# Expert gates: one-hot matrices built for 16 tokens at a time, token innermost, by bf16 tensor-tensor operations

## What is computed

```python
v1, i1 = lax.top_k(s1, PEER_TOPK_HALF)
v2, i2 = lax.top_k(s2, PEER_TOPK_HALF)
cand = (v1[..., :, None] + v2[..., None, :]).reshape(PEER_CHUNK, PEER_HEADS, -1)
cand_idx = (i1[..., :, None] * N_KEYS + i2[..., None, :]).reshape(PEER_CHUNK, PEER_HEADS, -1)
top_s, pos = lax.top_k(cand, PEER_TOPK)
experts = jnp.take_along_axis(cand_idx, pos, axis=-1)
gate = jax.nn.softmax(top_s.astype(jnp.float32), axis=-1).astype(hc.dtype)
u = jnp.take(expert_u, experts, axis=0)
act = jax.nn.gelu(jnp.einsum('chkd,cd->chk', u, hc))
v = jnp.take(expert_v, experts, axis=0)
return jnp.einsum('chk,chkd->cd', gate * act, v)
```

## Time and profile before

| | |
|---|---|
| median of three runs | 3415.33 us |
| lowest and highest | 3412.12, 3416.04 us |
| profiled execution, span from its first to its last instruction | 3404.0 us |
| median of the runs less that span | 11.3 us |
| TensorE busy in the span | 3128.4 us (92%) |
| VectorE busy | 2179.6 us (64%) |
| ScalarE busy | 1150.9 us (34%) |
| GpSimd busy | 1267.2 us (37%) |
| mean granted TensorE clock, share of full | 0.977 |

### The profile page before, as it was taken

One profiled execution on the slowest core, in us unless ns is written; L12 is line 12 of the kernel. 1 busy time (PEld: TensorE's weight loads), 2 busy tenths in 40 slices (PEclk: granted clock), 3 DMA queues, 4 the chain that ended last, 5 costly groups with the idle time before them and its releaser, 6 DMA issues.

```text
span 3404.0 us, 46182 instructions
## 1 busy us (share of the span) xinstructions
PE 3128.4 (92%) x14602; PEld 2508.8 (74%) x14602; DVE 2179.6 (64%) x4512; ACT 1150.9 (34%) x1478; POOL 1267.2 (37%) x513
## 2 busy tenths in 40 slices
PE   5888999998999999979999977788789999999998
PEld 3777788775678887757788866666668788888886
DVE  7973555133356623964169999999991566666664
ACT  3344322245332223323332234344443222222222
POOL 3313444432144444424434432222224344444442
PEclk8989999999999999989999999999999999999999
DMA  8411454421145442212234433444435555555552
GB/s 322 170 38 62 160 197 169 140 68 62 38 143 188 179 158 88 81 62 90 90 103 147 139 123 141 155 142 148 152 133 204 167 181 191 197 197 188 191 188 75
DMA packets 170247, 482.32 MB, mean 142 GB/s; under 512 B 15360, under 2 KB 48896, under 8 KB 168080
## 3 DMA queue, kind: packets, MB, share of 16 engines
q1 hardware_dynamic: 147680, 410.83, 35.6%
q10 hardware_dynamic: 22448, 70.14, 5.3%
HBM read 411.70 MB, written 69.21 MB: 141 GB/s over the span
## 4 chain that ended last, share of the span: by engine, by line
PE 41%; issue 35%; DVE 12%; POOL 10%; DVEq 1%; ACT 1%; DMA 0%; POOLq 0%; SPq 0%; ACTq 0%
PE ps L1614 39%; POOL w_lo L545 10%; DVE oh_key L1547 2%; DVE oh_gate L1544 2%; DVE oh_gate L1545 2%; PE pa L1614 2%; DVE oh_gate L1546 2%; DVE s_acc L1410 1%; DVE e_t L1568 1%; DVEq L1544 0%; DMA e_g<-expert_act 0%; DVE s_tmp L1461 0%; DVEq L1407 0%; DVE s_pb L1422 0%; DVE mg_lo L1463 0%
## 5 line engine op out<-in xcount | busy, mean ns | idle before, releaser
L545 POOL TENSOR_TENSOR w_lo<-raw,w_hi 128x1024 fp32r<-128x1024 f32 x509 | 1267.0, 2491 | 2105.7 <-ACT w_hi L562 2105.5
L1614 PE MATMUL ps<-h_hi,w_hi 128*128 128x512 f32 x2392 | 954.4, 399 | 43.8 <-ACT h_hi L641 36.9
L1614 PE MATMUL ps<-h_hi,w_lo 128*128 128x512 f32 x2392 | 942.9, 394 | 0.0
L1614 PE MATMUL ps<-h_lo,w_hi 128*128 128x512 f32 x2392 | 918.1, 391 | 0.0
L562 ACT ACTIVATE w_hi<-raw 128x1024 fp32r<-128x1024 f32 x509 | 537.6, 1058 | 718.3 <-PE ps L1614 593.4
L1614 PEld LDWEIGHTS ps<-h_hi,w_hi 128*128 128x128 f32 x2392 | 457.1, 191 | 147.2 <-issue 42.0
L1614 PEld LDWEIGHTS ps<-h_hi,w_lo 128*128 128x128 f32 x2392 | 455.7, 191 | 96.8
L1614 PEld LDWEIGHTS ps<-h_lo,w_hi 128*128 128x128 f32 x2392 | 452.6, 189 | 93.7 <-issue 1.7
L1614 PE MATMUL ps<-wa_hi,w_hi 128*128 128x512 f32 x1024 | 404.9, 395 | 5.7 <-DVE wa_lo L1571 5.7
L1614 PE MATMUL ps<-wa_lo,w_hi 128*128 128x512 f32 x1024 | 409.7, 400 | 0.0
L1614 PE MATMUL ps<-wa_hi,w_lo 128*128 128x512 f32 x1024 | 402.4, 393 | 0.0
(11 more groups left out here) (314 smaller groups left out, 3586.5 us busy)
## 6 DMA issues: line engine op xcount, KB each, us to landing
ada<-in_ada SPq DMA_DIRECT2D x144, 512.0 KB, 5.0
raw<-in_expert_u SPq DMA_DIRECT2D x128, 512.0 KB, 3.8
raw<-in_expert_v SPq DMA_DIRECT2D x128, 512.0 KB, 4.5
raw<-in_ffn_in SPq DMA_DIRECT2D x88, 512.0 KB, 4.2
expert_act<-g_act ACTq DMA_DIRECT2D x128, 256.0 KB, 3.1
gate_matrix<-w_st ACTq DMA_DIRECT2D x16, 2048.0 KB, 6.6
e_w<-gate_matrix SPq DMA_DIRECT2D x16, 2048.0 KB, 11.3
e_g<-expert_act SPq DMA_DIRECT2D x128, 256.0 KB, 8.0
```

Of the source, the lines that this page charges most:

```text
L545: nc.gpsimd.tensor_tensor(w_lo[:, k, :], raw[:, k, :], w_hi[:, k, :].bitcast(F32), ALU.subtract)\
L1614: return nc.tensor.matmul(out, a, b, start=start, stop=stop_)
```

## The change

The one-hot matrices are made for 16 tokens at once. The buffers are laid out [key, token] instead of [token, key], two buffers of 16 tokens each (`OHB`, `OHT`). For each 16 tokens VectorE compares an expanded iota with the first keys (`oh_hit`) and with the second keys (`oh_key`), both broadcast over the 128 keys, then multiplies `oh_hit` by each of the three gate parts. All operands are bf16; keys and gate parts are kept as bf16 (`r_key`, `r_gate`). TensorE waits for `oh_ready` once in 16 tokens, and both its operands now step over 16 elements (`[:, b, :, t]`, `[:, b, a, :, t]`). `oh_hits` orders the multiplications behind the comparison. `OH_FREE` is 8 groups, that is two buffers of 16 tokens.

```diff
@@ -59,7 +59,8 @@
 NG = NK // GE
 ADA0 = 8
 WTOK = 32
-OHG = 4
+OHT = 16
+OHB = 2
 U_FIRST, U_GATES = 44, 64
 U_LAST = NK - U_FIRST - U_GATES
 
@@ -273,11 +274,12 @@
     r_q = ar("r_q", 0, [2 * PH, S])
     w_st = ar("w_st", 0, [2, NK, WTOK])
     r_s = ar("r_s", 32 * K, [TT, 2 * PH, NK])
-    oh_gate = ar("oh_gate", 32 * K, [4 * OHG, 3, NK], BF16)
-    oh_key = ar("oh_key", 44 * K, [4 * OHG, NK], BF16)
-    r_rest = ar("r_rest", 48 * K, [S])
-    r_part = ar("r_part", 50 * K, [S], BF16)
-    iota_b = ar("iota_b", 51 * K, [NK], BF16)
+    oh_gate = ar("oh_gate", 32 * K, [OHB, 3, NK, OHT], BF16)
+    oh_key = ar("oh_key", 56 * K, [OHB, NK, OHT], BF16)
+    oh_hit = ar("oh_hit", 64 * K, [OHB, NK, OHT], BF16)
+    iota_t = ar("iota_t", 72 * K, [NK, OHT], BF16)
+    r_key = ar("r_key", 76 * K, [2, S], BF16)
+    r_gate = ar("r_gate", 78 * K, [3, S], BF16)
     r_w = ar("r_w", 64 * K, [2 * PH, NK])
     r_oh = ar("r_oh", 64 * K, [PH, TK, TK])
     r_cand = ar("r_cand", 72 * K, [PH, TK * TK])
@@ -293,7 +295,7 @@
     r_z = ar("r_z", 92 * K, [2, TT, PH])
 
     g_act = at("g_act", ada_off, [2, S])
-    r_T = at("r_T", ada_off + 4 * K, [4, S])
+    r_T = at("r_T", ada_off + 4 * K, [2, S])
 
     wa_hi = ar("wa_hi", 0, [2, GE, S], F32R)
     wa_lo = ar("wa_lo", 32 * K, [2, GE, S], F32R)
@@ -356,7 +358,7 @@
         sem(n) for n in ("mix_done", "pw_mm", "pmh", "pml", "mgh", "mgt", "mg_done"))
     rs_mm, rs_out, top_done, gx_done, gate_done, rt_mm, rt_done = (
         sem(n) for n in ("rs_mm", "rs_out", "top_done", "gx_done", "gate_done", "rt_mm", "rt_done"))
-    oh_ready, wb_mm, wb_free = (sem(n) for n in ("oh_ready", "wb_mm", "wb_free"))
+    oh_hits, oh_ready, wb_mm, wb_free = (sem(n) for n in ("oh_hits", "oh_ready", "wb_mm", "wb_free"))
     act_st = [sem(f"act_st{i}") for i in range(2)]
     w_out_st = [sem(f"w_out_st{i}") for i in range(2)]
     e_w_in = sem("e_w_in")
@@ -926,6 +928,8 @@
     assert U_FIRST % RING == U_GATES % RING == U_LAST % RING == 0
     WPER = 2 * U_GATES // (S // WTOK)
 
+    OH_FREE = OHB * OHT // 4
+
     def act_peer(act, hi):
         m, T = M0["query"], T0["query"]
         act.wait_ge(h_ready, 6 * DT)
@@ -955,8 +959,9 @@
             hi.upto(m + k + 3)
             act_gelu(act, 0, RING, m, T, k, 0)
         act.wait_ge(rt_mm, 1)
-        for a in range(3):
-            nc.scalar.activation(r_T[:, a, :], pa[:, a, :], ACT.Copy).then_inc(rt_done, 1)
+        for a in range(2):
+            nc.scalar.activation(r_key[:, a, :], pa[:, a, :], ACT.Copy).then_inc(rt_done, 1)
+        nc.scalar.activation(r_T[:, 0, :], pa[:, 2, :], ACT.Copy).then_inc(rt_done, 1)
         act.wait_ge(rt_done, 3)
         nc.scalar.activation(r_z[:, 0, 0, 0:1], r_z[:, 1, 0, 0:1], ACT.Copy).then_inc(wb_free, 4)
         for k in range(U_FIRST - RING // 2, U_FIRST):
@@ -972,7 +977,7 @@
                 n = WTOK // 4 // (WPER // 2)
                 for q in range(n * (k % (WPER // 2)), n * (k % (WPER // 2)) + n):
                     g = WTOK // 4 * b + q
-                    act.wait_ge(wb_mm, i * (2 * WTOK // 4) + (OHG + g + 1))
+                    act.wait_ge(wb_mm, i * (2 * WTOK // 4) + (OH_FREE + g + 1))
                     if q == 0 and not isinstance(i, int):
                         act.wait_ge(w_out_st[b], i * 16)
                     nc.scalar.activation(w_st[:, b, :, 4 * q:4 * q + 4].rearrange("p n t -> p t n"),
@@ -1526,32 +1531,31 @@
         step(v.reciprocal(z1, z0))
         v.tensor_tensor(e, e, bc(z1, 2, TK), ALU.mult).then_inc(gate_done, 1)
 
-        step(v.tensor_copy(iota_b[:, :], iota))
+        v.tensor_copy(iota_t[:, :, :], bc(iota, 2, OHT))
         dve.wait_ge(rt_done, 3)
-        step(v.tensor_copy(r_part[:, :], r_T[:, 2, :]))
-        step(v.tensor_tensor(r_T[:, 3, :], r_T[:, 2, :], r_part[:, :], ALU.subtract))
-        step(v.tensor_copy(r_part[:, :], r_T[:, 3, :]))
-        step(v.tensor_tensor(r_rest[:, :], r_T[:, 3, :], r_part[:, :], ALU.subtract))
-
-        per = 2 * WTOK // 4
+        step(v.tensor_copy(r_gate[:, 0, :], r_T[:, 0, :]))
+        step(v.tensor_tensor(r_T[:, 1, :], r_T[:, 0, :], r_gate[:, 0, :], ALU.subtract))
+        step(v.tensor_copy(r_gate[:, 1, :], r_T[:, 1, :]))
+        step(v.tensor_tensor(r_T[:, 0, :], r_T[:, 1, :], r_gate[:, 1, :], ALU.subtract))
+        step(v.tensor_copy(r_gate[:, 2, :], r_T[:, 0, :]))
+
+        per = 2 * WTOK // OHT
         with dve.Fori(0, S // (2 * WTOK)) as i:
-            for g in range(per):
-                dve.wait_ge(wb_mm, i * per + (g + 1))
-                for j in range(4):
-                    s = g % OHG * 4 + j
-                    tok = i * (2 * WTOK) + (4 * g + j)
-                    key1, key2, gate, less1 = (r_T[:, a, bass.ds(tok, 1)] for a in range(4))
-                    v.tensor_scalar(oh_gate[:, s, 0, :], iota_b[:, :], key1, gate, ALU.is_equal, ALU.mult)
-                    v.tensor_scalar(oh_gate[:, s, 1, :], iota_b[:, :], key1, less1, ALU.is_equal, ALU.mult)
-                    v.tensor_scalar(oh_gate[:, s, 2, :], iota_b[:, :], key1, r_rest[:, bass.ds(tok, 1)], ALU.is_equal, ALU.mult)
-                    ins = v.tensor_scalar(oh_key[:, s, :], iota_b[:, :], key2, None, ALU.is_equal)
+            for n in range(per):
+                b, tok = n % OHB, bass.ds(i * (2 * WTOK) + OHT * n, OHT)
+                dve.wait_ge(wb_mm, (i * per + (n + 1)) * (OHT // 4))
+                v.tensor_tensor(oh_hit[:, b, :, :], iota_t[:, :, :], bc(r_key[:, 0, tok], 1, NK), ALU.is_equal).then_inc(oh_hits, 1)
+                v.tensor_tensor(oh_key[:, b, :, :], iota_t[:, :, :], bc(r_key[:, 1, tok], 1, NK), ALU.is_equal)
+                dve.wait_ge(oh_hits, i * per + (n + 1))
+                for a in range(3):
+                    ins = v.tensor_tensor(oh_gate[:, b, a, :, :], oh_hit[:, b, :, :], bc(r_gate[:, a, tok], 1, NK), ALU.mult)
                 ins.then_inc(oh_ready, 1)
 
     def dve_peer(dve):
         v = nc.vector
         dve_router(dve)
         m, T = M0["expert_v"], T0["expert_v"]
-        dve.wait_ge(wb_mm, OHG + S // 4)
+        dve.wait_ge(wb_mm, OH_FREE + S // 4)
 
         def gated(g, k, b, i=None):
 
@@ -1981,7 +1985,7 @@
             for t in range(TT):
                 last = nc.tensor.transpose(pa[:, a, t * P:(t + 1) * P], r_i[:, a, t, :], ident)
                 if a == t == 0:
-                    last.then_inc(wb_mm, OHG)
+                    last.then_inc(wb_mm, OH_FREE)
         last.then_inc(rt_mm, 1)
         for k in range(U_FIRST - RING // 2, U_FIRST):
             first(m, T, k, 0, RING)
@@ -1991,12 +1995,13 @@
                 first(m, T, k, i, WPER)
                 n = 2 * WTOK // 4 // WPER
                 for g in range(n * k, n * k + n):
-                    pe.wait_ge(oh_ready, i * (2 * WTOK // 4) + (g + 1))
+                    if 4 * g % OHT == 0:
+                        pe.wait_ge(oh_ready, i * (2 * WTOK // OHT) + (4 * g // OHT + 1))
                     pe.wait_ge(wb_free, i * (2 * WTOK // 4) + (g + 1))
                     for j in range(4):
-                        s, out = g % OHG * 4 + j, pa[:, g % 4, j * NK:(j + 1) * NK]
+                        b, t, out = 4 * g // OHT % OHB, (4 * g + j) % OHT, pa[:, g % 4, j * NK:(j + 1) * NK]
                         for a in range(3):
-                            last = mm(out, oh_key[:, s, :], oh_gate[:, s, a, :], a == 0, a == 2)
+                            last = mm(out, oh_key[:, b, :, t], oh_gate[:, b, a, :, t], a == 0, a == 2)
                     last.then_inc(wb_mm, 1)
         m, T = m + U_GATES, T + U_GATES
         with pe.Fori(0, U_LAST // RING) as i:
```

## The result

The changed kernel takes 3713.89 us (median of four runs, 3711.86 to 3716.56) against 3413.72 for the kernel before, run beside it four times: a ratio of 1.0881, 95% interval [1.0868, 1.0894]. It is slower by 300 us. The prediction had it slower too, but by 125 us.

A forecast was written before the change was run, and what follows sets the result against it. VectorE was taken to bound the 572.3 us gate stage. With strided gate matmuls TensorE would need 1536 x 0.227 + 1536 x 0.227 = 697 us, +125 on the median 3415.33, giving 3540 us; range 3345 to 3650.

The forecast's parts named there:

- What bounds the kernel before: Gate stage: VectorE sets the pace, busy 560.80 of 572.30 us; TensorE needs 433, so 139 us is the most to gain.
- VectorE's new cost: Gate stage: five bf16 tensor-tensor operations per 16 tokens, 10.0 to 15.7 us with GpSimd blocks, expected near the lower end.
- Set-up and the first 16 tokens: Start of gate stage: larger iota, one more cast, first matrices after 16 tokens; cost 0 to 5 us once, taken as 0.
- The step that decides, a lone element at 1.77 ns: Gate matmuls: 128 elements 32 bytes apart each cost a 16-byte read, so 0.227 us a matmul instead of 0.055.
- The ratio reading (0.10): Gate matmuls: ScalarE's factor of 1.84 makes 0.055 into 0.10 us, kernel 3345 us; chance of 0.10 to 0.12: 0.16.
- the free step: Gate matmuls: the step costs nothing, 0.055 us each, kernel 3276 us with a fast VectorE; chance 0.10.
- The weight load hidden behind the matmul: Gate matmuls: 0.227 us taken; weight load and moving operand sharing the pace would make 0.454, +474 us, 3889, chance 0.04.
- "TensorE without a pause": Gate stage: 1536 fp32r and 1536 gate matmuls, each at 0.227 us, back to back, 697 us.
- rival 2: Gate stage: clock falls during strided matmuls; one low stretch per tile, 8 matmuls x 0.2, adds 102 us: 3642; chance 0.26.
- rival 1: The 1536 gate matmuls: TensorE's read path absorbs the step, wholly or at twice the time, below 0.146 us; faster, chance 0.26.
- Rival 3: Gate stage: the change doesn't relieve VectorE, 16 tokens again take 17.9 us, no change in time; chance 0.02.
- the time around the profiled span: Whole kernel: median run 3415.33 us against profiled span 3404.0, 11.3 more, left as it is.

The follow-up runs named there:

- runs of 2: Changed kernel with tokens innermost in runs of 2 instead of 16, elements 4 bytes apart: 3286.04 us, ratio 0.9625 to the kernel before.
- three orders of equal work: Changed kernel with strided gate and fp32r matmuls alternating by three, by twelve, or by 24 (unaltered): 3595.66, 3674.12 and 3713.89 us.
- runs of 8: Changed kernel with tokens innermost in runs of 8 instead of 16, elements 16 bytes apart: 3667.18 us.

## Why the prediction was right or wrong

- **What bounds the kernel before: right.** In the kernel with runs of 2, VectorE's new operations wait 173 us for TensorE and the stage falls to 442 us; 130 us were gained there, 139 were named as the most.
- **VectorE's new cost: right**, at the faster end: 1.22 us an operation. The stage has 249 us of it, 7.8 per 16 tokens, under the 10.0 named. Set-up and the first 16 tokens held nothing up.
- **The step that decides, a lone element at 1.77 ns: right.** 0.233 us a gate matmul for 0.227. The six thousandths are 1536 x 0.006 = 9 us. The steps of 16, 8 and 4 bytes show the mechanism, 16 bytes at a time, in the way that it was put. The ratio reading (0.10) was wrong, the free step too. That ScalarE's rows gave nearly the same amount, 1.81 ns, lent the choice weight; no run shows that the two have one cause, and it may be luck.
- **The weight load hidden behind the matmul: right**, 0.063 us with it alone.
- **"TensorE without a pause" at 0.227 us per fp32r matmul: this is the step that failed.** The sum held the clock at 2.4 GHz and put its fall into rival 2, with chance 0.26. It fell in every tile: the tile's 24 fp32r matmuls took 8.03 us and not 5.45, and 64 x 2.58 = 165 us. With the 9 above that is 697 + 174 = 871, for 869 measured. Of the 165 some 14 are not the clock's: behind strided gate matmuls the first fp32r matmul has 0.44 us instead of 0.227 at 2.4 GHz too, a change between the two kinds that the sum put at nothing. The clock's own part is some 151 us.
- **Rival 2's size was also too small.** It priced a low stretch of 3.42 us per tile, copied from one place in the trace before, 8 matmuls, +102 us and 3642. Here each was 6.8 us long, and twelve matmuls of each tile lay in it. The argument against it ("TensorE would hold instructions all the time") has fallen: TensorE's busy share is 100% in the changed stage, and its clock fell nevertheless. A busy share does not say how much the engine does in it: 24 strided gate matmuls and 24 fp32r ones last nearly the same (5.59 and 5.45 us), with 128 and 512 columns each. In the rows before the clock was low behind a stretch with little work; I took the idle time for the reason, and no row there said so.
- **The range's upper end, 3650, was therefore 64 us too low.** It took in the strided price and the clock together, at rival 2's 3642, but with the low stretch mis-sized.
- **A slip in rival 1:** at 0.110 us the stage would be 348.5 + 169 = 517.5 us and the kernel 3361, not 3357; nothing else rests on it.
- Rival 3 has nothing for it. That the time around the profiled span stays 11.3 us was a poor basis: the changed kernel's profiled execution has 3712.6 us of span and took 3714.47, so 1.9 lie around it; if that held before too, the execution traced there took some 3406 us.

## What to carry to other kernels

A layout that makes one engine's writes cheap is read by another: count, for a matmul's moving operand, how many of its elements share 16 bytes, since each 16 bytes took some 1.8 ns here, and four bf16 elements in them were enough. Both engines could be served at once, with runs of two tokens: 4-byte pairs gave VectorE its fast pace (1.22 for 2.28 us) and TensorE its dense one (0.057 us). And a slow stretch of matmuls may also cost behind it: in it the gate matmuls took 273 us more than dense ones (1536 x 0.178), and 1.2 GHz for the next tile's first twelve matmuls added some 151.

## What the runs showed of the hardware

- The moving operand's pace: 16 bytes in 1.77 ns by the mean of a run, at steps of 16 (0.227 us) and 8 bytes (0.115) alike, and not contradicted at 4 (0.057). The spacing of strided matmuls is the same at both levels of the clock (0.240 and 0.241 us), while fp32r ones go from 0.227 to 0.427. The Trainium skill's "Advanced Engine Details and Errata" (SBUF Cachelines) asks for at least two hits on a 16-byte line. The lines agree; the two do not for this operand: with two elements per line a matmul still takes twice its dense time, and the dense pace took four.
- A weight load of 128 bf16 columns with elements 32 bytes apart takes 148 ns for 98, and nearly all of it is hidden (0.063 us a matmul for 0.055).
- The clock fell with TensorE busy 100% of the time. The three orders of equal work show that the arrangement decides (1.00, 0.86 and 0.75). What it is about a long piece of strided matmuls that brings it, no run here separates; that the same cause acts in the kernel before fits, and wasn't tried.
- The stage of the changed kernel ran in step with the clock, 6.8 us low and 6.8 high to a tile of 13.6. With tiles a little shorter (runs of 8: 12.9 us) more of the fp32r matmuls kept 2.4 GHz. Whether being in step makes the loss larger was not tested by itself.
- Changing between groups of three strided bf16 and three fp32r matmuls costs 0.08 us per pair of groups beyond the mean prices. The first fp32r matmul behind strided gate matmuls is followed by the next after 0.44 us, behind dense ones after 0.31, for 0.227. Its cause is open.
